# Two gate chunks of each layer's embedding gate streamed 512 columns wide instead of 256

## The reference

```python
        h = h + mix
        h = h + swiglu(rms_norm(h, norm_ffn[i]), ffn_w_in[i], ffn_w_out[i])
        gate = jax.nn.sigmoid(rms_norm(h, ple_norm[i]) @ ple_w_gate[i])
        h = h + gate * (p[i] @ ple_w_proj[i])
    return h
```

## Time and profile before

| | |
|---|---|
| median of 3 runs | 1050.77 us (1050.7 to 1050.96) |
| the profiled execution | 1051.27 us |
| its span, first to last instruction | 1049.5 us |
| PE busy | 1040.1 us, 99% of the span, 6552 matmuls |
| PE weight load busy | 921.1 us, 88% |
| DVE, ACT, POOL busy | 728.4, 595.8, 57.3 us |
| granted PE clock | 1.000 of full speed, mean |

### The profile page before, as it was taken

The page is one execution under the profiler, slowest core; times in us unless marked ns, Lnnn a source line. Parts: engine busy times, 40 slices in busy tenths (PEclk is TensorE's granted clock), DMA queues, the critical chain, the costliest instruction groups (busy, mean ns, idle before and its releaser), DMA issues.

```text
span 1049.5 us, 16130 instructions
## 1 busy us (share of the span) xinstructions
PE 1040.1 (99%) x6552; PEld 921.1 (88%) x6552; DVE 728.4 (69%) x852; ACT 595.8 (57%) x754; POOL 57.3 (5%) x53
## 2 busy tenths in 40 slices
PE   9999999999999999999999999999999999999998
PEld 8998999888888889888888888899998888888888
DVE  6888877565565568965666666677988676666664
ACT  5677545554444457765644444576776664444464
POOL 0000001200000030002006000010000200000010
PEclk9999999999999999999999999999999999999999
DMA  9536354646556545455556555455524465455651
GB/s 337 196 123 198 121 201 142 201 161 208 193 166 216 180 141 201 130 181 179 158 197 207 188 177 201 164 194 163 162 81 156 135 200 201 160 203 185 212 163 41
DMA packets 131273, 184.30 MB, mean 176 GB/s; under 512 B 3200, under 2 KB 107904, under 8 KB 131200
## 3 DMA queue, kind: packets, MB, share of 16 engines
q1 hardware_dynamic: 130752, 182.68, 52.0%
q0 software_dynamic: 160, 0.52, 0.2%
q10 hardware_dynamic: 288, 0.07, 0.0%
HBM read 182.21 MB, written 1.05 MB: 175 GB/s over the span
## 4 chain that ended last, share of the span: by engine, by line
PE 92%; DVE 3%; ACT 3%; issue 1%; DMA 1%; SPq 0%; DVEq 0%; ACTq 0%
PE PS L406 90%; PE PS L414 2%; ACT WH L1209 1%; DVE WL L1802 1%; DMA RAW<-in_gla_w_in_dram 1%; DMA H<-in_x_dram 0%; DVE AR L2262 0%; ACT AR L1223 0%; ACT H L1511 0%; DVE AR L2260 0%; ACT AR L1684 0%; DVE AR L2254 0%; ACT X L1217 0%; ACT HS L1223 0%; DVE SC L1840 0%
## 5 line engine op out<-in xcount | busy, mean ns | idle before, releaser
L1802 DVE TENSOR_TENSOR WL<-RAW,WH 128x2048 fp32r<-128x2048 f32 (+1 forms) x170 | 374.9, 2210 | 116.7 <-ACT WH L1209 116.3
L1209 ACT ACTIVATE WH<-RAW 128x2048 fp32r<-128x2048 f32 (+1 forms) x177 | 326.4, 1849 | 84.5 <-PE PS L406 73.9
L406 PE MATMUL PS<-WH,X 128*128 128x512 f32 (+1 forms) x1168 | 306.4, 345 | 0.6 <-issue 0.4
L406 PE MATMUL PS<-O,WH 128*128 128x512 f32 (+1 forms) x880 | 265.8, 363 | 0.2 <-DVE WL L1802 0.2
L406 PEld LDWEIGHTS PS<-WH,X 128*128 128x128 f32 x1168 | 204.2, 189 | 27.5 <-issue 2.6
L406 PE MATMUL PS<-X,WH 128*128 128x256 f32 (+1 forms) x864 | 217.1, 330 | 0.8 <-ACT WH L1209 0.8
L406 PE MATMUL PS<-O,WL 128*128 128x256 f32 x744 | 203.1, 281 | 0.0
L406 PE MATMUL PS<-WL,X 128*128 128x512 f32 (+1 forms) x584 | 200.4, 343 | 0.0
L406 PEld LDWEIGHTS PS<-O,WH 128*128 128x128 f32 x880 | 155.8, 189 | 25.4 <-issue 0.7
L406 PE MATMUL PS<-X,WL 128*128 128x256 f32 x608 | 166.4, 281 | 0.1
L406 PEld LDWEIGHTS PS<-X,WH 128*128 128x128 f32 x864 | 144.8, 190 | 15.6 <-ACT WH L1209 1.1
(11 more groups left out here) (218 smaller groups left out, 778.9 us busy)
## 6 DMA issues: line engine op xcount, KB each, us to landing
RAW<-in_ffn_w_in_dram SPq DMA_DIRECT2D x44, 1024.0 KB, 5.1
RAW<-in_w_ff_dram SPq DMA_DIRECT2D x32, 1024.0 KB, 5.4
RAW<-in_ffn_w_out_dram SPq DMA_DIRECT2D x22, 1024.0 KB, 5.1
RAW<-in_w_in_dram SPq DMA_DIRECT2D x20, 1024.0 KB, 5.2
RAW<-in_gla_w_in_dram SPq DMA_DIRECT2D x12, 1024.0 KB, 5.4
RAW<-in_diff_w_in_dram SPq DMA_DIRECT2D x12, 1024.0 KB, 5.1
RAW<-in_ple_w_gate_dram SPq DMA_DIRECT2D x8, 1024.0 KB, 5.2
RAW<-in_w_out_dram SPq DMA_DIRECT2D x4, 1024.0 KB, 5.0
```

The source lines that it names most:

```text
L406: return e.matmul(o, l, r, start=start, stop=stop, skip_group_check=skip)
L1209: act(high, raw, ACT.Copy).then_inc(s["w_hi"], 1)
L1802: e.tensor_tensor(low, raw, high.bitcast(F32), ALU.subtract).then_inc(s["w_lo"], 1)
```

## The change

The list of chunks gets the gate's first 512 columns as two long chunks (c and c+1, by halves of the contraction), and the last 512 stay two wide chunks (c+2, c+3). `toks_long` does c and c+1 in banks 3 and 4, with the turning steps of `pn0` and `pn1` asked for by the same table. The sigmoid, the multiply and the add for these columns are done by token half, 512 columns at a time, instead of by 256 columns of both halves. In layer 0 the steps of `nm1` come later: 0 and 1 after c+2, 2 and 3 in the middle of c+3, 4 and 5 after it. The waits on `ple_h` follow, SP's for the output among them.

```diff
@@ -109,7 +109,8 @@
                 tall(f"ple_w_proj{layer}", 0)
             if i >= 1:
                 tall(f"ffn_w_out{layer}", i - 1)
-        for i in range(4):
+        long(f"ple_w_gate{layer}", 0)
+        for i in range(2, 4):
             wide(f"ple_w_gate{layer}", 256 * i)
     return out
 
@@ -435,7 +436,7 @@
     def h_step(name, k):
 
         if name == "nm1":
-            e.wait_ge(s["ple_h"], k // 2 + 1)
+            e.wait_ge(s["ple_h"], max(k // 2 + 1, 2))
         elif k in (0, 4):
             e.wait_ge(s["res"], 4 * NEXT.index(name) + (2 if k == 0 else 4))
         turn_step(name, m.tok(m.H), k)
@@ -1018,17 +1019,27 @@
             i.then_inc(s["ple_t" if tb == 0 else "gemm"], 1)
 
     def ple(layer):
-        r0 = 16 if layer == 0 else 24
-        for n in range(4):
-            if n == 1:
-                e.wait_ge(s["res"], r0)
-            if layer == 1 and n == 3:
-                last_gates()
-                break
-            toks(AT[f"ple_w_gate{layer}"] + n, 3 + n, m.pair("OX"[layer]), f"pn{layer}" if n == 0 else None)
-            if layer == 0 and n >= 1:
-                h_step("nm1", 2 * n - 2)
-                h_step("nm1", 2 * n - 1)
+
+        c, ops = AT[f"ple_w_gate{layer}"], m.pair("OX"[layer])
+
+        def free(tb):
+            if tb:
+                e.wait_ge(s["res"], 24 if layer else 16)
+
+        for x in range(2):
+            toks_long(c + x, x, (3, 4), ops, (0, 1), f"pn{layer}", free)
+        toks(c + 2, 5, ops)
+        if layer:
+            last_gates()
+            return
+        for k in (0, 1):
+            h_step("nm1", k)
+        toks(c + 3, 6, ops, None, range(4))
+        for k in (2, 3):
+            h_step("nm1", k)
+        toks(c + 3, 6, ops, None, range(4, 8))
+        for k in (4, 5):
+            h_step("nm1", k)
 
     swiglu(0)
     ple(0)
@@ -1613,25 +1624,34 @@
         new_residual(5 if layer else 3, pn)
         rstd_y(pn)
         e.preload_act_table_set(SIGMOID)
-        for n in range(4):
-            c = AT[f"ple_w_gate{layer}"] + n
-            hi(c + 2)
-            if layer == 1 and n == 3:
-                for tb in range(2):
-                    e.wait_ge(*((s["gemm"], c + 1) if tb else (s["ple_t"], 1)))
-                    act(g[:, tb, 768:1024], PS[:, 6 + tb, 0:256], ACT.Sigmoid, scale=r[:, tb:tb + 1]).then_inc(s["ple_g"], 1)
-                return
-            e.wait_ge(s["gemm"], c + 1)
+        c = AT[f"ple_w_gate{layer}"]
+        for tb in range(2):
+            hi(c + 2 + tb)
+            e.wait_ge(*((s["gemm"], c + 2) if tb else (s["long"], 8 + layer)))
             e.wait_ge(s["pn_r"], layer + 1)
+            act(g[:, tb, 0:512], PS[:, 3 + tb, :], ACT.Sigmoid, scale=r[:, tb:tb + 1]).then_inc(s["ple_g"], 1)
+        hi(c + 4)
+
+        def gates(n):
+            e.wait_ge(s["gemm"], c + n + 1)
             for tb in range(2):
                 i = act(g[:, tb, 256 * n:256 * n + 256], PS[:, 3 + n, 256 * tb:256 * tb + 256], ACT.Sigmoid,
                         scale=r[:, tb:tb + 1])
             i.then_inc(s["ple_g"], 1)
-            if layer == 0 and n >= 1:
-                turn_hi("nm1", 2 * n - 2, 2 * n - 1)
-                if n == 2:
-                    row_square("nm1", 0, 0)
-                    row_square("nm1", 1, 0)
+
+        gates(2)
+        if layer:
+            for tb in range(2):
+                e.wait_ge(*((s["gemm"], c + 4) if tb else (s["ple_t"], 1)))
+                act(g[:, tb, 768:1024], PS[:, 6 + tb, 0:256], ACT.Sigmoid, scale=r[:, tb:tb + 1]).then_inc(s["ple_g"], 1)
+            return
+        turn_hi("nm1", 0, 1)
+        hi(c + 5)
+        turn_hi("nm1", 2, 3)
+        row_square("nm1", 0, 0)
+        row_square("nm1", 1, 0)
+        gates(3)
+        turn_hi("nm1", 4, 5)
         e.preload_act_table_set(LOGEXP)
 
     swiglu(0)
@@ -2375,25 +2395,32 @@
         pn = f"pn{layer}"
         new_residual(5 if layer else 3, [4, 5, 6, 7], r)
         rows_rstd(pn, ("pn_r", layer + 1))
-        for n in range(4):
-            c = slice(256 * n, 256 * n + 256)
-            lo(AT[f"ple_w_gate{layer}"] + n + 2)
-            if layer == 1 and n == 3:
-                for tb in range(2):
-                    gg = v3(g, 2)[:, tb, c]
-                    e.wait_ge(s["ple_g"], 8 + tb)
-                    e.tensor_tensor(gg, gg, v3(pw, 2)[:, tb, c], ALU.mult).then_inc(own.up(), 1)
-                    settled()
-                    e.tensor_tensor(H[:, tb, c], H[:, tb, c], gg, ALU.add).then_inc(s["ple_h"], 1)
-                return
-            gg = v3(g, 2)[:, :, c]
-            e.wait_ge(s["ple_pw"], 4 * layer + 4)
-            e.wait_ge(s["ple_g"], 4 * layer + n + 1)
-            e.tensor_tensor(gg, gg, v3(pw, 2)[:, :, c], ALU.mult).then_inc(own.up(), 1)
+        c = AT[f"ple_w_gate{layer}"]
+        e.wait_ge(s["ple_pw"], 4 * layer + 4)
+
+        def gated(ready, tb, n, w):
+
+            t, cols = slice(tb, tb + 1) if tb is not None else slice(0, 2), slice(n, n + w)
+            gg = v3(g, 2)[:, t, cols]
+            e.wait_ge(s["ple_g"], ready)
+            e.tensor_tensor(gg, gg, v3(pw, 2)[:, t, cols], ALU.mult).then_inc(own.up(), 1)
             settled()
-            e.tensor_tensor(H[:, :, c], H[:, :, c], gg, ALU.add).then_inc(s["ple_h"], 1)
-            if layer == 0 and n >= 1:
-                turn_lo("nm1", 2 * n - 2, 2 * n - 1)
+            e.tensor_tensor(H[:, t, cols], H[:, t, cols], gg, ALU.add).then_inc(s["ple_h"], 1)
+
+        for tb in range(2):
+            lo(c + 2 + tb)
+            gated(4 * layer + tb + 1, tb, 0, 512)
+        lo(c + 4)
+        gated(4 * layer + 3, None, 512, 256)
+        if layer:
+            for tb in range(2):
+                gated(8 + tb, tb, 768, 256)
+            return
+        turn_lo("nm1", 0, 1)
+        lo(c + 5)
+        turn_lo("nm1", 2, 3)
+        gated(4, None, 768, 256)
+        turn_lo("nm1", 4, 5)
 
     ple(0, swiglu(0))
 
@@ -2687,7 +2714,7 @@
             piece(c, j)
     o_rows = m.out.rearrange("(b p) d -> p b d", p=128)
     for n in range(3):
-        e.wait_ge(s["ple_h"], 5 + n)
+        e.wait_ge(s["ple_h"], max(5 + n, 6))
         e.dma_start(o_rows[:, :, 256 * n:256 * n + 256], H[:, :, 256 * n:256 * n + 256]).then_inc(s["d_out"], 16)
     for b in range(2):
         e.wait_ge(s["ple_h"], 8 + b)
```

## The result

The changed kernel takes 1055.70 us (median of six, 1054.17 to 1056.16), the kernel before in the same sessions 1050.87 (six, 1050.70 to 1051.62). The ratio is 1.0041, 95% interval 1.0031 to 1.0051 (the two medians alone would give 1.0046): slower, as forecast. The medians are 4.8 us apart, more than the forecast 3.1 us, and 1055.70 lies 0.4 us above the top of the forecast's range (1052.3 to 1055.3). The six executions are not alike: four have a mean granted clock of 0.998 and take 1055.66 to 1056.16, two have 1.000 and take 1054.17 and 1054.49.

The account below looks back on a forecast made before the run. PE, busy 99% of the span, was taken to bound the kernel. Losses of 1.38 us (layer 0) and 1.75 us (layer 1) sum to 3.13, moving the median from 1050.77 to 1053.9 us; range 1052.3 to 1055.3.

Parts of the forecast that it names:

- part 1: Gate chunks c and c+1: 48 wide matmuls replace 96 narrow ones, giving back 0.64 us a layer if nothing else moves.
- part 2: Step 7 falls behind token half 1 of c, 2.58 us later; c+2's low part then ends at 698.99 in layer 0.
- The chain of 7.80: From step 7's transposes through ACT and DVE to the end of c+2's low part: 7.80 us, without slack inside.
- The spare time of 1.05 us: Before the change, c+2's low part was taken to be ready 1.05 us before PE needs it.
- part 3: PE ends c+1 at 696.85 and idles 2.29 us before c+2, which starts at 699.14; this swallows the 0.64 us gain.
- The 0.15 from low part to start: Before c+2, PE was to start 0.15 us after DVE's low part ends, as in the one measured wait.
- parts 4 and 5: Layer 0's next block (d0) starts 1.38 us later; layer 1's last matmul starts 1.75 us later.
- the slacks worked out for them: Layer 0 after c+2: DVE and ACT work ready before c+3 and step 3 (0.5 us to spare), and before step 6.
- the bounds of 0.60 and 0.84: ACT's sigmoid of 512 columns of one half: between 0.60 and 0.84 us, hidden behind DVE's split chain.
- a rival of 6%: The clock falls in the stall in one layer, costing 2.9 us over half a chunk: 1056.8 us; chance 6%.
- the reading of the tail: At the kernel's end the clock fell 2.8 us after the last matmul's end; the stall's 2.29 is a little less.
- The rival on the other side: c+2's split is on time, so PE does not wait: 1.5 us less than before, 1049.3; chance 8%.

Follow-up runs that it names:

- e1: The changed kernel with steps 6 and 7 of pn0 and pn1 both turned ahead of k = 3; 1049.74 us, ratio to before 0.9986.
- e2: The changed kernel, step 7 still late, but c+2's high and low parts made between steps 6 and 7; 1049.56 us, ratio to before 0.9985.
- e3: The changed kernel with eight unread 512-column matmuls between c+1 and c+2 in each layer; 1054.24 us, ratio to before 1.0030.
- e4: The changed kernel with layer 0's embedding and nm1 steps as before, so the change is in layer 1 alone; 1054.28 us, ratio to before 1.0029.
- e7: The changed kernel with three unread 512-column matmuls between c+1 and c+2 in each layer; 1054.24 us, ratio to before 1.0030.
- e5: The kernel before, narrow, with only step 7 of pn0 and pn1 moved to k = 6 of c; 1053.21 us, ratio to before 1.0020.

## Why the prediction was right, and where it fell short

**Wider matmuls (part 1): right in direction, the gain somewhat smaller.** In the changed kernel c and c+1 take 696.80 + 0.2267 - 685.05 = 11.98 us, where they took 697.46 - 685.01 = 12.45: 0.47 saved of the forecast 0.61, since each k with a turned step takes 0.92 and not 0.90, and the second chunk takes a little longer too. The stall hides this. In e1, with no stall, the time from the four transposes ahead of the first gate matmul (684.55) to the narrow matmul at 696.95, the second of c+2, is 12.40, and without the 0.12 of c+2's first start 12.28; before, from 684.66 to the 697.46 at which c+1 ended, 12.80: 0.52 saved.

**Step 7 moves (part 2): right.** Forecast 6.18 us after the first gate matmul and 2.58 later than before; measured 6.26. The missing 0.08 is the step between turned k: 0.92 (685.84, 686.76, 687.68), not 0.90. The chain of 7.80 behind it was 7.81. The spare time of 1.05 us is layer 1's: in layer 0 of the kernel before, steps 0 and 1 of nm1 stood between c+1 and c+2, and c+2 started only at 698.21. This changes nothing in the sum, since the new order puts c+2 right behind c+1. e2 shows that it is the order on ACT and DVE that costs.

**The stall (part 3): right.** Forecast 2.29 idle, shown 2.08 in both layers. The forecast counted from the end of the last start's 0.2267, while the row counts the idle time from the end of the matmul itself. Counted the forecast's way, from 696.80 + 0.2267 to c+2's start at 699.27 (forecast 699.14), it is 2.24. The 0.15 from low part to start held exactly.

**Layer 0 and layer 1 (parts 4 and 5): right.** 1.45 and 1.85 against 1.38 and 1.75, clock apart; the executions without a fall are 3.3 and 3.6 over the median before, e3 3.1, against 3.13. No new wait stood before c+3, at step 3 or at step 6, so the slacks worked out for them were enough. The sigmoid of 512 columns took 0.67, between the bounds of 0.60 and 0.84, and was hidden.

**The clock: the term that the sum lacked.** The prediction took the clock as a rival of 6%, because 2.29 us is less than the 2.8 us that PE had been idle in the tail before the fall, and left it out of the sum. It came in four of six executions, and adds 1.48 in the profiled one. The price for a fall, 2.9 us, was too high: a start took 0.213 and not up to 0.24, and the low clock ended inside c+2. The step that failed is the reading of the tail, which took the 2.8 us from PE's stop to the fall for the idle time that a fall needs. In layer 0 the fall came 2.8 us after PE's stop as well, but PE had been idle for only 2.08 of them and was working again. Nor does so long an idle time always bring a fall: in the tail of the changed kernel PE is idle from 1050.81 to the end of the span at 1054.4, 3.6 us, at a clock of 1.00.

```profile
1050.90:1053.90 3.00, 0.00 (x0) 0.00 (x0) 0.85 (x2) 0.42 (x1) 0.00 (x0) 1.00 0.13 44
1053.90:1054.40 0.50, 0.00 (x0) 0.00 (x0) 0.00 (x0) 0.00 (x0) 0.00 (x0) 1.00 0.00 0
```

What decides between a fall and none after the same idle time stays open. So 1053.9 holds for the executions without a fall (1054.2 and 1054.5), not for the median. The Trainium skill ("TensorE: Matmul & The Clock Gate", Part 1: The HAM clock gate) names two states, half and full, with an idle PE going to half. The rows agree on the states, 0.50 and 1.00; the idle times at 1.00 in layer 1 and in this tail show that an idle PE doesn't always go to half.

**The rival on the other side: right in its price.** "The split is on time after all" was priced at 1.5 us under before; e1 and e2, which bring it about in two ways, are 1.4 and 1.6 under, a difference between the two that their intervals don't tell apart.

## What to carry to other kernels

When a loop is reordered, look at what else is issued by its index: here a table keyed by k moved one transpose by a whole token half, behind which two other engines, working strictly in order, had the next weights to prepare. Find the chain behind each moved step and its spare time (1.05 us in layer 1 here) before counting what the faster matmuls give back. A stall of a dense PE has two prices, the wait and the clock that it may lose, and the second varies from execution to execution: compare the granted clock of every run, not of the profile alone.

## What was not expected of the hardware

After an idle time of 2.08 us between dense matmuls the granted clock fell to 0.50 in layer 0 of the profiled execution, at a cost of 1.48 us, and it stayed at 1.00 after the same idle time in layer 1. The fall came 0.7 us after PE had begun to work again. Four of six executions have a mean clock of 0.998 and are about 1.6 us longer than the others, both with two such gaps (the changed kernel) and with one (e4). That fits one fall in each: the lost clock of the profiled one, 1.5 + 0.19 + 0.02 by the stretches above, about 1.7 of 1054 us, is 0.0016. Which of the two gaps it follows in the unprofiled ones is not known. With the longest idle time there cut to 1.42 or 0.29 us (e7, e3; both in layer 1), and with one of 0.92 (e5), the mean clock was 0.999 or 1.000 in all of six, six and ten executions.
